# Expert groups: the up product in two halves, additions as two float32r terms, slots released by counts

## The chip, the cores and the metric

The kernel runs on one core of a Trainium2 chip. The metric is the device time of one execution of the whole program, in microseconds (us). The core has TensorE (PE) for matrix products, VectorE (DVE), ScalarE (ACT), GpSimd (POOL), and SyncE (SP), whose queue issues most of the loads from HBM. The loads of all queues are moved by the same 16 DMA engines.

## What is computed

The program is one step of a small diffusion trunk on 384 tokens (128 of a prompt, 256 of a sample) of width 1024, in two layers. Layer 0 mixes tokens by a long convolution, layer 1 by attention. Each is followed by a mixture of 16 experts of 512 hidden units, of which every token uses two, and this is where the change lies:

```python
def _hier_moe(x, w_group, b_group, w_expert, b_expert, w_up, w_down):
    ...
    for e in range(N_EXPERTS):
        a, b = jnp.split(t @ w_up[e], 2, axis=-1)
        y = y + combine[:, e:e + 1] * ((jax.nn.silu(a) * b) @ w_down[e])
    return y.reshape(B, L, D)
```

After the experts of a layer come a residual and a layer norm; layer 1 begins with a modulation by vectors that are a product of a condition with `w_ada`. All data is float32.

## The kernel before

Every engine has its own program, written out by hand, and semaphores order them. The order on each engine is the order of the code.

**Loads.** All large weights go through slots of 2 MB. SP issues them in the order of `LOAD_ORDER`, and each waits until its slot's last user is done. For a layer's experts there are 48 pieces of 2 MB (`MOE_W`): for each expert the two halves of `w_up` over the rows (c = 0, 1) and `w_down` (c = 2). Six ring slots and five places that are free at that time hold 11 pieces, so pieces 0 to 10 are loaded while the stages ahead of the experts still run, and piece i, from 11 on, waits until piece i - 11 has been used. For an up piece that wait (`wait_used`) is for `up_ready`, counted in groups, for a down piece for `expert_done`. `piece` (line 522) and `load` (line 505) issue the transfers. Behind the experts of layer 0 the same slots take `cond7` and `cond8` (two column blocks of `w_ada` for layer 1), then `qkv_4` and so on, through `wait_slot_free`, which waits for `expert_done` too.

**Groups.** The tokens of an expert are dealt out in groups of 32 slots (`SLOT_TOK`); an expert has one or more groups, and `expert` runs a hardware loop over them. In this trace there are 33 groups in each layer. The rows of a group are gathered from HBM by POOL (`group_row`, 128 KB each), turned by DVE into `xgT`. On PE a group is three steps, all through the helper `mm` (line 812):

1. up: 32 float32 products of `xgT` (128x32, held in the array) with 256 columns of `w_up`, in four column strips of the array, into bank 0; the trace shows two instructions for each float32 product, so 64.
2. add (`combine`): the result of the previous group is added to the 384 token rows, which stay in banks 2 to 7. The result is split into three bfloat16 terms (`y3`) whose sum is exact, and multiplied by a 0/1 matrix `ohT` that spreads the slots over the tokens: 3 token tiles x 3 terms x 4 strips = 36 products.
3. down: 16 float32 products (32 instructions) of `heT` with `w_down`, into bank 1.

Between 1 and 3 ACT takes the silu of one half of bank 0 (`gated`, tile `sa`), DVE multiplies it by the other (`he`) and turns it (`heT`). After 3, DVE scales bank 1 by the gates (`yv`) and makes the three terms. After an expert's last group a tiny product (`mm` on `ident`) raises `expert_done`. After the last group `combine_last` adds its result, and the layer norm follows: DVE's statistics (`st`, line 2149), then ACT and DVE on each token tile. In layer 0, ACT's program has the copies of the `cond7` and `cond8` products (`cond_rows_copied`) between these tiles.

## Time and profile before

| what | value |
|---|---|
| time, median of 3 runs | 1043.76 us (1041.48 to 1048.89) |
| span of the profiled execution, first to last instruction | 1041.7 us |
| the fastest timed run, for what lies around the span | 1041.48 us |
| busy: PE, DVE, ACT, POOL | 983.5, 699.0, 189.6, 195.2 us |
| moved from and to HBM | 318.29 MB |
| expert groups: layer 0, layer 1 | about 296 to 517 us, about 791 to 1025 us |

The page gives no other time for the profiled execution than its span, and the fastest timed run is 0.2 us away from it, so the sum is made against 1041.7 us, which is 2.1 us below the median. Lines are those of the kernel before. "Share" of the DMA engines is a mean over 16 of them (the profiler's figure goes slightly over 1), the granted clock is 1.00 at 2.4 GHz and 0.50 at 1.2 GHz.

### The profile page before, as it was taken

The page shows a single profiled execution, that of the slowest core. Times are in us where ns is not written, and L with a number is a line of the kernel's source. Part 1 is how long each engine was busy: PE and PEld are TensorE (multiplying, and loading weights), DVE is VectorE, ACT ScalarE, POOL GpSimd, SP SyncE. Part 2 cuts the span into 40 slices and gives each one's busy share as a digit, 9 for nine tenths or more (in the row PEclk, how much of TensorE's full clock was granted, in tenths as well). Part 3 has the DMA queues.
Part 4 walks back from the last instruction along what each step waited for, and adds up shares of the span by engine and source line. Part 5 has one row for each costly group of instructions (what it writes and reads, how often), then busy time and mean ns, then how long its engine had stood idle before and what let it go on. Part 6 is the DMA issues. An engine that isn't in the chain of part 4 may idle for free.

```text
span 1041.7 us, 28193 instructions
## 1 busy us (share of the span) xinstructions
PE 983.5 (94%) x11412; PEld 583.7 (56%) x11412; DVE 699.0 (67%) x1771; ACT 189.6 (18%) x443; POOL 195.2 (19%) x304
## 2 busy tenths in 40 slices
PE   8999999999899999999899999999989999999783
PEld 2555556565556656666555554575555655666451
DVE  6458884956766666666679995474676666666457
ACT  4342233012310000000140013462231000000003
POOL 1500000620132222222100001254013222222111
PEclk9999999999899999999989999999989999999896
DMA  9964666950999999999997588832097999999991
GB/s 331 400 258 162 221 243 223 389 186 25 344 340 405 405 406 406 405 405 405 393 402 256 213 327 321 289 102 74 5 357 284 374 405 406 405 404 405 407 373 64
DMA packets 102208, 318.29 MB, mean 306 GB/s; under 512 B 8403, under 2 KB 12691, under 8 KB 101748
## 3 DMA queue, kind: packets, MB, share of 16 engines
q1 hardware_dynamic: 92228, 298.87, 74.7%
q0 software_dynamic: 5776, 17.30, 5.0%
q10 hardware_dynamic: 4128, 1.05, 0.4%
q8 instruction: 56, 0.92, 0.4%
q14 instruction: 20, 0.16, 0.0%
HBM read 311.44 MB, written 5.77 MB: 305 GB/s over the span
## 4 chain that ended last, share of the span: by engine, by line
PE 76%; DMA 8%; DVE 6%; SPq 6%; issue 2%; POOL 1%; ACT 1%; DVEq 0%; POOLq 0%
PE bank L812 74%; SPq L522 5%; DMA ring<-in_moe_w_down 4%; DMA ring<-in_w_ada 2%; POOL P L780 1%; PE bank L1320 1%; DVE P L2212 1%; DMA group_row<-token_rows,rows_now 1%; DVE st L2149 0%; PE bank L1027 0%; PE bank L859 0%; ACT x L1514 0%; DVE x L2263 0%; SPq L532 0%; PE bank L871 0%
## 5 line engine op out<-in xcount | busy, mean ns | idle before, releaser
L812 PE MATMUL bank<-ring,xgT 128*32 128x256 f32 x4224 | 244.0, 382 | 7.3 <-DMA ring<-in_moe_w_up 4.9
L812 PE MATMUL bank<-hT,ring 128*128 128x384 f32 x640 | 207.2, 486 | 0.0
L812 PEld LDWEIGHTS bank<-ring,xgT 128*32 128x32 f32 x4224 | 145.5, 111 | 87.6 <-issue 9.5
L812 PEld LDWEIGHTS bank<-hT,ring 128*128 128x128 f32 x640 | 121.4, 190 | 85.6 <-issue 1.8
L1722 DVE CUSTOM_DVE_ANT_0 ring<-ring,ring 128x1024 f32<-128x1024 f32 x112 | 137.1, 1224 | 3.4
L812 PE MATMUL bank<-ring,heT 128*32 128x256 f32 x2112 | 130.3, 386 | 5.3 <-DMA ring<-in_moe_w_down 5.0
L1557 ACT ACTIVATE sa<-bank 128x128 f32<-128x128 f32 x66 | 18.3, 277 | 425.0 <-PE bank L812 425.0
L812 PEld LDWEIGHTS bank<-ring,heT 128*32 128x32 f32 x2112 | 63.5, 110 | 56.4 <-DVE heT L2108 16.1
L2106 DVE TENSOR_TENSOR he<-sa,bank 128x128 f32<-128x128 f32 x66 | 19.0, 288 | 98.5 <-ACT sa L1557 98.5
L812 PE MATMUL bank<-y,ohT 32*128 32x256 bf16 x2448 | 81.3, 271 | 2.6 <-DVE y L2129 1.9
L746 POOL DMA_INDIRECT group_row<-token_rows,rows_now x68 | 74.0, 1088 | 17.6 <-issue 17.3
L812 PEld LDWEIGHTS bank<-y,ohT 32*128 32x128 bf16 x2448 | 56.2, 93 | 36.7 <-issue 27.7
L743 POOL COPY rows_now<-list_i 128x1 int32 (+1 forms) x68 | 12.4, 182 | 321.0 <-DVE xgT L2036 316.0
L2127 DVE TENSOR_TENSOR yv<-bank,slot_gate 128x256 f32<-128x256 f32 x66 | 28.0, 425 | 55.3 <-PE bank L812 55.3
L812 PE MATMUL bank<-ring,hT 128*128 128x512 f32 x96 | 46.8, 623 | 0.0
L812 PE MATMUL bank<-ring,yT 128*128 128x512 f32 x96 | 41.9, 593 | 1.0 <-DVE yT L1875 1.0
L812 PE MATMUL bank<-ring,qT 128*128 128x512 f32 x96 | 42.0, 593 | 0.8 <-DVE qT L2232 0.8
L2118 DVE SCALAR_TENSOR_TENSOR ohT<-pos_all,srow,oh_first 128x384 bf16<-128x384 f32 x66 | 40.4, 612 | 0.2 <-issue 0.2
L684 POOL TENSOR_TENSOR Y<-Y,tmp 128x512 f32<-128x512 f32 x6 | 7.6, 1274 | 145.4 <-DVE tmp L1846 145.1
L1462 ACT ACTIVATE zt<-bank,first 128x128 f32<-128x128 f32 (+1 forms) x48 | 17.5, 416 | 85.4 <-PE bank L812 85.4
L2121 DVE SCALAR_TENSOR_TENSOR slot_gate<-gate_s,slot_weight,slot_gate 128x256 f32<-128x256 f32 x66 | 31.6, 478 | 0.0
L1816 DVE SCALAR_TENSOR_TENSOR acc<-zt,first,acc 128x385 f32<-128x385 f32 x14 | 8.7, 620 | 34.1 <-ACT acc L1452 33.7
(299 smaller groups left out, 1193.8 us busy)
## 6 DMA issues: line engine op xcount, KB each, us to landing
ring<-in_moe_w_up SPq DMA_DIRECT2D x64, 2048.0 KB
ring<-in_moe_w_down SPq DMA_DIRECT2D x32, 2048.0 KB
ring<-in_k_ada SPq DMA_DIRECT2D x14, 2048.0 KB
ring<-in_w_ada SPq DMA_DIRECT2D x10, 2048.0 KB
ring<-in_na_w_qkv SPq DMA_DIRECT2D x6, 2048.0 KB
ring<-in_hy_w_in SPq DMA_DIRECT2D x5, 2048.0 KB
ring<-in_hy_w_out SPq DMA_DIRECT2D x2, 2048.0 KB
ring<-in_na_w_out SPq DMA_DIRECT2D x2, 2048.0 KB
```

The source lines that it names most:

```text
L522: sp.dma_start(w_view(i, 4, 1024), src.rearrange("o (k p) n -> p (o k) n", p=128)).then_inc(w_loaded[W_SLOT[i]], 16)
L743: nc.gpsimd.tensor_copy(rows_now[b][:], list_i[:, column]).then_inc(S["rows_named"], 1)
L746: nc.gpsimd.indirect_dma_start(out=group_row[b][:, :], out_offset=None, in_=token_rows[l][:, :], in_offset=bass.IndirectOffsetOnAxis(ap=ro ...
L780: nc.gpsimd.tensor_scalar_mul(p, p, den[:, 2 * u:2 * u + 1]).then_inc(scaled[0], 1)
L812: return nc.tensor.matmul(out, lhsT, rhs, start=first, stop=last)
L1462: last = nc.scalar.activation(zt[:, n % 2, at_:at_ + b - a], ps[bank_of(g)][:, a:b], ACT.Identity, bias=VT[:, V_BIN + n:V_BIN + n + 1])
L1557: nc.scalar.activation(sa[:], ps[0][:, 0:128], ACT.Silu).then_inc(S["sa_ready"], 1)
L1722: ins = v.tensor_tensor_reduce(scratch, w_view(i, 4, D)[:, q, :], cond_rows(l)[:, c * D:(c + 1) * D], 1.0, 0.0, ALU.mult, ALU.add, mod[l][ ...
L2106: v.tensor_tensor(he[:], sa[:], ps[0][:, 128:256], ALU.mult).then_inc(S["he_ready"], 1)
L2118: v.scalar_tensor_tensor(out=ohT[:].rearrange("p t n -> p (t n)"), in0=pos_all[:, 1, :], scalar=srow[:], in1=oh_first[:], op0=ALU.is_equal ...
L2121: v.scalar_tensor_tensor(out=slot_gate[:], in0=gate_s[:, 1, :], scalar=weight[1], in1=slot_gate[:], op0=ALU.mult, op1=ALU.add).then_inc(S[ ...
L2127: v.tensor_tensor(yv[:], ps[1][:, 0:256], slot_gate[:], ALU.mult).then_inc(S["y_step"], 1)
```

## The change

The inner units of an expert are taken in two halves h. The up product of half h has 128 columns and goes to bank h, so 64 products in place of 32; ACT and DVE handle a half (64 columns) as soon as it is there. Bank 1 is also that of the down product, so half 1 waits until DVE has read the previous group's result (`y_step`), and the down product waits until DVE has read half 1 (`he_ready`); it then starts on the units of half 0 when their `heT` is there. The result is split into two terms in float32r (`yt`) in place of three in bfloat16, and `ohT` becomes float32r too: 24 products in place of 36, and two DVE operations fewer. The tiny product and `expert_done` go; every slot is released by a count of groups (`piece_used`), on `up_ready` or `y_ready`; SP reads a count once for an expert and keeps it. Two tiles are cleared by DVE instead of one by POOL, and PE waits for `srow_ready` ahead of the first group.

```diff
+TERMS, Y_STEPS = 2, 4
-        y3 = at("y3", [128, 3, 256], RM + 10496, b16)
+        yt = at("yt", [128, 2, 256], RK + 3072, f32r)
+        ohT = at("ohT", [128, TT, 128], RM + 10496, f32r)
...
+            def piece_used(l, i):
+                e, c = divmod(i, 3)
+                if e not in groups_through[l]:
+                    count_groups(l, e)
+                if c == 2:
+                    sp.wait_ge(moe_sems[l]["y_ready"], groups_through[l][e])
+                else:
+                    sp.wait_ge(moe_sems[l]["up_ready"], groups_through[l][e] * 2)
...
                     if m <= j < m + MOE_W:
-                        sp.wait_ge(expert_done[l], (j - m) // 3 + 1)
+                        piece_used(l, j - m)
...
+                for e in range(EXPERTS - 4, EXPERTS):
+                    if e not in groups_through[l]:
+                        count_groups(l, e)
...
-                sp.wait_ge(expert_done[l], EXPERTS - 1)
+                piece_used(l, max(i for i in range(MOE_W) if W_SLOT[W_AT[f"moe{l}"] + i] == RING + 2))
...
-                nc.gpsimd.memset(y3[:], 0.0).then_inc(S["y3_ready"], 1)
-                nc.gpsimd.memset(ohT[:], 0.0).then_inc(S["ohT_ready"], 1)
+                nc.gpsimd.memset(ohT[:].bitcast(f32), 0.0).then_inc(S["ohT_ready"], 1)
...
-                        last = mm(bank_at(t, o), ohT[32 * o:32 * o + 32, t, :], y3[32 * o:32 * o + 32, term, :], False,
-                                  end and r + o % 2 >= 2 and term == 2)
+                        last = mm(bank_at(t, o), ohT[32 * o:32 * o + 32, t, :], yt[32 * o:32 * o + 32, term, :], False,
+                                  end and r + o % 2 >= 2 and term == TERMS - 1)
...
-                        for k in range(KT):
-                            if k % 4 == 0:
-                                wait_piece(k // 4)
-                            w = wup[k // 4][:, k % 4, :].rearrange("p (g q n) -> p q g n", q=4, n=32)
-                            for q in range(4):
-                                last = mm(ps[0][32 * q:32 * q + 32, 0:256].rearrange("s (g n) -> s g n", n=32),
-                                          xgT[:, k, :], w[:, q, :, :], k == 0, k == KT - 1)
-                        last.then_inc(S["up_ready"], 1)
+                        for h in range(2):
+                            if h == 1:
+                                pe.wait_ge(S["y_step"], before * Y_STEPS + 3)
+                            for k in range(KT):
+                                if h == 0 and k % 4 == 0:
+                                    wait_piece(k // 4)
+                                w = wup[k // 4][:, k % 4, :].rearrange("p (c h g q n) -> p q h c g n", c=2, h=2, g=2, q=4)
+                                for q in range(4):
+                                    last = mm(ps[h][32 * q:32 * q + 32, 0:128].rearrange("s (c g n) -> s c g n", c=2, g=2),
+                                              xgT[:, k, :], w[:, q, h, :, :, :], k == 0, k == KT - 1)
+                            last.then_inc(S["up_ready"], 1)
-                        pe.wait_ge(S["y3_ready"], w1)
+                        pe.wait_ge(S["yt_ready"], w1)
...
-                        pe.wait_ge(S["heT_ready"], w1)
+                        pe.wait_ge(S["he_ready"], before * 2 + 2)
                         wait_piece(2)
                         for q in range(4):
+                            if q % 2 == 0:
+                                pe.wait_ge(S["heT_ready"], before * 2 + 1 + q // 2)
                             for o in range(4):
                                 last = mm(ps[1][32 * o:32 * o + 32, 0:256], heT[:, 32 * q:32 * q + 32],
-                    mm(ps[0][0:2, 0:2], ident[:, 0:2], ident[:, 0:2]).then_inc(expert_done[l], 1)
...
                 pe.wait_ge(nb_ready, l + 1)
+                pe.wait_ge(S["srow_ready"], 1)
...
                 def gated(g):
-                    act.wait_ge(S["up_ready"], g + 1)
-                    nc.scalar.activation(sa[:], ps[0][:, 0:128], ACT.Silu).then_inc(S["sa_ready"], 1)
+                    for h in range(2):
+                        act.wait_ge(S["up_ready"], g * 2 + 1 + h)
+                        nc.scalar.activation(sa[:, 64 * h:64 * h + 64], ps[h][:, 0:64], ACT.Silu).then_inc(S["sa_ready"], 1)
...
+                v.memset(yt[:].bitcast(f32), 0.0).then_inc(S["yt_ready"], 1)
+                v.memset(credit[:, 2:3], 0.0).then_inc(S["y_step"], Y_STEPS)
...
+                def half_gated(g, h):
+                    cols_of = slice(64 * h, 64 * h + 64)
+                    dve.wait_ge(S["sa_ready"], g * 2 + 1 + h)
+                    v.tensor_tensor(he[:, cols_of], sa[:, cols_of], ps[h][:, 64:128], ALU.mult).then_inc(S["he_ready"], 1)
+                    dve.wait_ge(S["he_ready"], g * 2 + 1 + h)
+                    v.transpose(heT[:, cols_of], he[:, cols_of]).then_inc(S["heT_ready"], 1)
...
+                    step = g * Y_STEPS + Y_STEPS
+                    half_gated(g, 0)
                     dve.wait_ge(S["srow_ready"], g + 1)
                     v.tensor_scalar(oh_first[:], pos_all[:, 0, :], srow[:], None, ALU.is_equal).then_inc(S["oh_first_ready"], 1)
                     weight = [slot_weight[:, c, bass.ds(g, 1)] for c in range(2)]
                     v.tensor_scalar(slot_gate[:], gate_s[:, 0, :], weight[0], None, ALU.mult).then_inc(S["y_step"], 1)
+                    half_gated(g, 1)
+                    dve.wait_ge(S[f"rows{b}_in"], count * 16)
+                    turned(group_row[b][:])
...
                     v.tensor_tensor(yv[:], ps[1][:, 0:256], slot_gate[:], ALU.mult).then_inc(S["y_step"], 1)
-                    dve.wait_ge(S["y_step"], g * 6 + 3)
-                    v.tensor_copy(y3[:, 0, :], yv[:]).then_inc(S["y_step"], 1)
-                    dve.wait_ge(S["y_step"], g * 6 + 4)
-                    v.tensor_tensor(yv[:], yv[:], y3[:, 0, :], ALU.subtract).then_inc(S["y_step"], 1)
-                    dve.wait_ge(S["y_step"], g * 6 + 5)
-                    v.tensor_copy(y3[:, 1, :], yv[:]).then_inc(S["y_step"], 1)
-                    dve.wait_ge(S["y_step"], g * 6 + 6)
-                    v.tensor_tensor(y3[:, 2, :], yv[:], y3[:, 1, :], ALU.subtract).then_inc(S["y3_ready"], 1)
+                    dve.wait_ge(S["y_step"], step + 3)
+                    v.tensor_copy(yt[:, 0, :], yv[:]).then_inc(S["y_step"], 1)
+                    dve.wait_ge(S["y_step"], step + 4)
+                    v.tensor_tensor(yt[:, 1, :], yv[:], yt[:, 0, :], ALU.subtract).then_inc(S["yt_ready"], 1)
```

How PE's instructions stand in an expert's loop (layer 0, second expert; `ring_53` and `ring_56` are its up pieces, `ring_49` its down piece; ISA, REGISTER_ALU and branches are the sequencer's). Before:

```order
L812 MATMUL bank<-ring_53,xgT 32x256 x16
L812 MATMUL bank<-ring_56,xgT 32x256 x16
L812 MATMUL bank<-y_136,ohT 128x256 x24
L1106 ISA
L812 MATMUL bank<-y_136,ohT 128x256 x12
L812 MATMUL bank<-ring_49,heT 32x256 x16
L1144 REGISTER_ALU
L1144 COMPARE_AND_BRANCH
L812 MATMUL bank<-first 2x2
```

After:

```order
L823 MATMUL bank<-ring_53,xgT 32x128 x16
L823 MATMUL bank<-ring_56,xgT 32x128 x16
L1160 ISA
L823 MATMUL bank<-ring_53,xgT 32x128 x16
L823 MATMUL bank<-ring_56,xgT 32x128 x16
L823 MATMUL bank<-yt,ohT 128x256 x16
L1117 ISA
L823 MATMUL bank<-yt,ohT 128x256 x8
L1173 ISA
L1177 REGISTER_ALU
L823 MATMUL bank<-ring_49,heT 32x256 x16
L1155 REGISTER_ALU
```

The up product now stands twice, with 128 columns in place of 256, the additions are 24 in place of 36, the tiny product behind the loop is gone, and sequencer instructions with a wait stand ahead of half 1 and of the down product.

DVE's instructions of one group (layer 0, the second group; `y_136` is `y3`). Before:

```order
L2106 TENSOR_TENSOR he<-sa,bank 128x128
L2108 STREAM_TRANSPOSE heT<-he 128x128
L2036 STREAM_TRANSPOSE xgT<-group_row_130 128x256
L2113 TENSOR_SCALAR oh_first<-pos_all,srow 128x384
L2115 TENSOR_SCALAR slot_gate<-gate_s,slot_weight 128x256
L2118 SCALAR_TENSOR_TENSOR ohT<-pos_all,srow,oh_first 128x384
L2121 SCALAR_TENSOR_TENSOR slot_gate<-gate_s,slot_weight,slot_gate 128x256
L2123 TENSOR_SCALAR srow<-srow 128x1
L2127 TENSOR_TENSOR yv<-bank,slot_gate 128x256
L2129 CAST y_136<-yv 128x256
L2131 TENSOR_TENSOR yv<-yv,y_136 128x256
L2133 CAST y_136<-yv 128x256
```

After:

```order
L2126 TENSOR_TENSOR he<-sa,bank 128x64
L2128 STREAM_TRANSPOSE heT<-he 128x64
L2135 TENSOR_SCALAR oh_first<-pos_all,srow 128x384
L2137 TENSOR_SCALAR slot_gate<-gate_s,slot_weight 128x256
L2126 TENSOR_TENSOR he<-sa,bank 128x64
L2128 STREAM_TRANSPOSE heT<-he 128x64
L2053 STREAM_TRANSPOSE xgT<-group_row_130 128x256
L2144 SCALAR_TENSOR_TENSOR ohT<-pos_all,srow,oh_first 128x384
L2147 SCALAR_TENSOR_TENSOR slot_gate<-gate_s,slot_weight,slot_gate 128x256
L2149 TENSOR_SCALAR srow<-srow 128x1
L2153 TENSOR_TENSOR yv<-bank,slot_gate 128x256
L2155 CAST yt<-yv 128x256
```

The multiplication and the turn come in two pieces, with two operations on slot numbers between them; the turn of the next group's rows (`xgT`) stands behind the second piece; the splitting behind `yv` is two operations shorter.

SP's queue at the end of the experts of layer 0, where the first load behind them is `cond7` (`in_w_ada`); TENSOR_LOAD reads a count of groups. Before:

```order
L522 ISA
L522 DMA ring_52<-in_moe_w_up 128x4x1024
L532 TENSOR_LOAD NBi
L532 ISA x2
L522 ISA
L522 DMA ring_53<-in_moe_w_down 128x4x1024
L505 DMA ring_49<-in_w_ada 128x8x512
```

After:

```order
L489 TENSOR_LOAD NBi
L489 ISA x2
L500 REGISTER_ALU
L539 ISA
L539 DMA ring_53<-in_moe_w_down 128x4x1024
L489 TENSOR_LOAD NBi
L489 ISA x2
L489 TENSOR_LOAD NBi
L489 ISA x2
L489 TENSOR_LOAD NBi
L489 ISA x2
L522 DMA ring_49<-in_w_ada 128x8x512
```

Three counts are read between the last expert piece and the load of `cond7`; the order of the loads themselves is as before.

## Rows read from the trace of the kernel before

**Rows 1.** The page: busy time, share of the span and instructions of each engine.

```profile
PE 983.5 (94%) x11412; PEld 583.7 (56%) x11412; DVE 699.0 (67%) x1771; ACT 189.6 (18%) x443; POOL 195.2 (19%) x304
```

**Rows 2.** Windows, expert stages: length, busy time by engine; last, clock, DMA share, GB/s.

```profile
300.00:520.00 220.00, 216.11 (x4380) 132.43 (x4376) 145.55 (x435) 10.96 (x36) 47.44 (x97) 1.00 1.03 404
810.00:1012.00 202.00, 193.14 (x3834) 117.15 (x3825) 124.59 (x375) 8.04 (x29) 41.59 (x85) 0.97 1.02 405
799.00:809.00 10.00, 9.98 (x216) 5.92 (x208) 7.17 (x23) 0.55 (x2) 1.66 (x5) 1.00 0.14 39
```

**Rows 3.** The chain that ended last, in order of time: start, length, what.

```profile
495.37 25.58 DMA ring<-in_w_ada
521.09 3.81 PE bank L812 x32
...
989.13 23.81 DMA ring<-in_moe_w_down
```

**Rows 4.** Timeline, PE in late layer 1: start, length, [idle before and what ended it].

```profile
927.82 3.66 PE L812 MATMUL bank<-ring,xgT 128*32 128x256 f32 x64
931.41 1.16 PE L812 MATMUL bank<-y,ohT 32*128 32x256 bf16 x36
932.53 1.93 PE L812 MATMUL bank<-ring,heT 128*32 128x256 f32 x32
934.28 3.64 PE L812 MATMUL bank<-ring,xgT 128*32 128x256 f32 x64
...
940.74 0.19 PE L812 MATMUL bank<-first 128*2 128x2 f32 x2
...
970.37 3.27 PE L812 MATMUL bank<-ring,xgT 128*32 128x256 f32 x32 [2.82 <-DMA ring<-in_moe_w_up]
...
997.04 3.59 PE L812 MATMUL bank<-ring,heT 128*32 128x256 f32 x32 [2.53 <-DMA ring<-in_moe_w_down]
...
1013.08 1.93 PE L812 MATMUL bank<-ring,heT 128*32 128x256 f32 x32 [1.42 <-DMA ring<-in_moe_w_down]
```

**Rows 5.** Timeline, ACT and DVE in the first of these groups.

```profile
931.54 0.28 ACT L1557 ACTIVATE sa<-bank 128x128 f32<-128x128 f32 x1 [6.41 <-PE bank L812]
931.85 0.29 DVE L2106 TENSOR_TENSOR he<-sa,bank 128x128 f32<-128x128 f32 x1 [1.36 <-ACT sa L1557]
932.17 0.31 DVE L2108 STREAM_TRANSPOSE heT<-he 128x128 f32<-128x128 f32 x1
...
935.15 0.42 DVE L2127 TENSOR_TENSOR yv<-bank,slot_gate 128x256 f32<-128x256 f32 x1 [0.79 <-PE bank L812]
```

**Rows 6.** PE's rows nearest to the new shapes: timeline, chain, groups by form.

```profile
763.64 1.08 PE L812 MATMUL bank<-first,mod 128*32 128x128 f32 x32
...
36.19 2.68 PE bank L851 x24
...
L812 PEld LDWEIGHTS bank<-y,ohT 32*128 32x128 bf16 x2448 | 56.2, 93 | 36.7 <-issue 27.7 <-PE bank L812 2.8 <-DVE y L2129 2.1
```

**Rows 7.** Timeline, SP's queue: start, length of the issue.

```profile
488.61 12.16 SPq L505 DMA_DIRECT2D ring<-in_w_ada  x2
...
807.33 0.37 SPq L522 DMA_DIRECT2D ring<-in_moe_w_down  x1
```

**Rows 8.** ACT behind layer 0's experts (timeline); two stretches with a low clock (windows).

```profile
521.00 1.45 ACT L1514 ACTIVATE x<-bank,sd 128x512 f32<-128x512 f32 x2 [0.55 <-DVE sd L1889]
...
523.07 0.60 ACT L1386 ACTIVATE arow<-bank 128x512 f32<-128x512 f32 x1 [0.62 <-PE bank L812]
...
526.00:533.00 7.00, 6.24 (x16) 3.46 (x15) 4.70 (x18) 4.43 (x11) 0.00 (x0) 0.51 1.02 407
998.00:1000.00 2.00, 2.00 (x24) 1.00 (x20) 0.00 (x0) 0.00 (x0) 0.00 (x0) 0.50 1.03 410
```

**Rows 9.** Timeline, DVE on the third term of layer 1's last group.

```profile
1022.86 0.29 DVE L2133 CAST y<-yv 128x256 bf16<-128x256 f32 x1
1023.19 0.43 DVE L2135 TENSOR_TENSOR y<-yv,y 128x256 bf16<-128x256 f32 x1
```

More of the change, by code:

```diff
@@ L220, in build @@
 def build(nc, A, y_prompt, y_sample, new_k, new_v):
-    f32, i32, b16 = mybir.dt.float32, mybir.dt.int32, mybir.dt.bfloat16
+    f32, i32, b16, f32r = mybir.dt.float32, mybir.dt.int32, mybir.dt.bfloat16, mybir.dt.float32r
     ACT = mybir.ActivationFunctionType
@@ L379, in build @@
         w_loaded = [sem(f"w_loaded{r}") for r in range(RING + EXTRA)]
-        expert_done = [sem(f"expert_done{l}") for l in range(DEPTH)]
         group_ready = sem("group_ready")
@@ L418, in build @@
                 "oh_pair", "oh_ready", "gathered", "picks_ready", "list_summed", "list_ready", "hot_ready", "picks_step", "rows_named", "rows_stored", "x_added", "rows0_in", "rows1_in", "xgT_ready", "up_ready", "sa_ready",
[L419 removed]
+                "he_ready", "heT_ready", "y_ready", "y_step", "yt_ready", "oh_first_ready", "ohT_ready", "srow_ready", "combined")})
         block = ctx.enter_context(nc.Block())
@@ L483, in last_group, with count_groups @@
                         return G_AT["qk"] + 4 * s + 3 if s < 4 else G_AT["v_01" if s == 4 else "v_12"]
+            groups_through = [{}, {}]
+            def count_groups(l, e):
+                groups = sp.value_load(NBi[0:1, NB_CUM + 1 + e:NB_CUM + 2 + e], min_val=1, max_val=MAX_BLOCKS)
+                groups_through[l][e] = whole_pairs(groups) if e == EXPERTS - 1 else groups
+            def piece_used(l, i):
[6 more added lines that the diff above has]
+                    sp.wait_ge(moe_sems[l]["up_ready"], groups_through[l][e] * 2)
             def wait_slot_free(i):
@@ L525, in experts @@
                 S = moe_sems[l]
-                def wait_used(i):
-                    e, c = divmod(i, 3)
-                    if c == 2:
-                        sp.wait_ge(expert_done[l], e + 1)
-                    else:
-                        groups = sp.value_load(NBi[0:1, NB_CUM + 1 + e:NB_CUM + 2 + e], min_val=1, max_val=MAX_BLOCKS)
-                        sp.wait_ge(S["up_ready"], groups)
                 for i in range(MOE_W):
@@ L548, in experts @@
                     if i >= RING + EXTRA:
-                        wait_used(i - RING - EXTRA)
+                        piece_used(l, i - RING - EXTRA)
                     elif slot < RING:
@@ L1106, in combine @@
                             pe.wait_ge(S["combined"], done)
-                        for term in range(3):
+                        for term in range(TERMS):
                             last = add_term(r, term)
@@ L1113, in combine_last @@
                 def combine_last(total):
-                    for term in range(3):
-                        if term < 2:
-                            pe.wait_ge(S["y_step"], total * 6 + 2 * term - 2)
+                    for term in range(TERMS):
+                        if term < TERMS - 1:
+                            pe.wait_ge(S["y_step"], total * Y_STEPS + 2 * term + 4)
                         else:
-                            pe.wait_ge(S["y3_ready"], total + 1)
+                            pe.wait_ge(S["yt_ready"], total + 1)
                         if term > 0:
@@ L1125, in combine_last @@
                             last = add_term(r, term, True)
-                            if term < 2 or r == 0:
+                            if term < TERMS - 1 or r == 0:
                                 last.then_inc(S["combined"], 1)
@@ L2101, in moe @@
                 total = dve.value_load(NBi[0:1, NB_ALL:NB_ALL + 1], min_val=EXPERTS, max_val=MAX_BLOCKS)
-                def group(g, b, count):
-                    dve.wait_ge(S["sa_ready"], g + 1)
-                    v.tensor_tensor(he[:], sa[:], ps[0][:, 128:256], ALU.mult).then_inc(S["he_ready"], 1)
-                    dve.wait_ge(S["he_ready"], g + 1)
-                    v.transpose(heT[:], he[:]).then_inc(S["heT_ready"], 1)
-                    dve.wait_ge(S[f"rows{b}_in"], count * 16)
-                    turned(group_row[b][:])
+                def half_gated(g, h):
[4 more added lines that the diff above has]
+                    v.transpose(heT[:, cols_of], he[:, cols_of]).then_inc(S["heT_ready"], 1)
+                def group(g, b, count):
+                    step = g * Y_STEPS + Y_STEPS
+                    half_gated(g, 0)
                     dve.wait_ge(S["srow_ready"], g + 1)
@@ L2119, in group @@
                                            in1=oh_first[:], op0=ALU.is_equal, op1=ALU.add).then_inc(S["ohT_ready"], 1)
-                    dve.wait_ge(S["y_step"], g * 6 + 1)
+                    dve.wait_ge(S["y_step"], step + 1)
                     v.scalar_tensor_tensor(out=slot_gate[:], in0=gate_s[:, 1, :], scalar=weight[1], in1=slot_gate[:],
```

6 lines of the change are left out of this document (2 added, 4 removed).

## The prediction

> **What bounds the kernel now.** I read the page's busy shares first, then the chain, then the expert stages by windows, and last PE and SP in order of time. The page makes PE the bound: it is busy 94% of the span [rows 1]. The windows of the two expert stages say otherwise. From 300 to 520 us and from 810 to 1012 us all 16 DMA engines are busy without a gap (share 1.03 and 1.02, 404 and 405 GB/s), while PE is busy for 216.1 of 220 and 193.1 of 202 us [rows 2]. Both are full; what counts is which of them the end waits for. The chain names it twice: cond8, a load behind the expert pieces of layer 0, from 495.37 to 521.09, and the last expert piece of layer 1 from 989.13 on [rows 3]. SP shows why these take 24 and 26 us, for 2 MB, which at 405 GB/s take 5.2: each is in a queue behind others. cond7 and cond8 are issued at 488.61, with the issue itself held up for 12.16 us [rows 7], so the slot was free long before the engines came to it. And at the end of layer 1 PE stands in front of pieces that have not landed: 2.82 us at 970, 2.53 at 997, 1.42 at 1013 [rows 4].
>
> The bytes give the same end. In layer 1 the engines are nearly idle from 799 to 809 (share 0.14) [rows 2], because piece 11 may not be issued before the third group of the first expert is through its up product, at 807.33 [rows 7]. From there 37 pieces of 2.097 MB and 33 gathers of 0.131 MB are 81.9 MB, 202 us at 405 GB/s: from 810 to 1012, and the last down product starts at 1013.08 [rows 4]. So PE's work in the expert stages is paid for only where it releases piece 11, and behind the last piece.
>
> **The change, part by part.** Take the group of rows 4 at 927.82: up to 931.41 (3.59 us), additions to 932.53 (1.12), down to 934.28 (1.75), together 6.46; after an expert's last group the tiny product adds 0.19, which over 16 experts and 33 groups is 0.09 a group. PE's work in a layer is 33 x 6.55 = 216 us.
>
> *Up in halves.* The same columns, in twice as many instructions. The nearest row has the shape of a half exactly: a 128x32 operand held, 128 columns moving, float32; 32 of them take 1.08 us [rows 6], and with some 0.28 for one to run through that is 26 ns each. 128 of them are 0.28 + 127 x 0.026 = 3.6 us, as the 64 before (3.66) [rows 4]. I take 0; bounds -0.1 and +0.3 (64 more instructions with 5 ns of overhead).
> *Half 1 waits for bank 1.* The wait is for `yv`, which in these rows ends at 935.57, 1.29 us after the up product began at 934.28 [rows 4, 5]; half 1 begins 1.8 us after it. Queued behind it on PE are half 1, the additions and the down product, and behind those ACT and DVE; 0.5 us of margin, so 0.
> *Two terms.* 24 products instead of 36, at the pace of the 36 (1.16 us with 0.27 for the last to run through: 25 ns each) 0.85 us, 0.3 less [rows 4]. No row shows a float32r product. From below it is bounded by that; from above by loading the held operand, 128 columns of float32, one after the other: transposes with such an operand take 2.68 us for 24 [rows 6]. I take 0.85: the strips of the additions lie in different rows of the array, and the bfloat16 loads take 93 ns each where 36 of them go through in 1.16 us, so they do overlap by strip [rows 4, 6].
> *The down product's start.* Before, it waits for `heT`, ready at 932.48, when the additions end, too [rows 4, 5]. Now the additions would end 0.3 earlier, at 932.24; half 1's `he` is ready by 0.28 + 0.29 and two hand-overs after 931.54, at 932.14 even if 64 columns took as long as 128, and half 0's `heT` is long there. Down follows the additions; 0.3 gained. DVE has two operations more for the halves (at most 0.6 us) and 0.72 us fewer for the third term [rows 5, 9]; it doesn't matter.
> *The tiny product and the counts.* -0.09 a group on PE. SP reads three counts ahead of cond7's load; the queue it feeds runs some 25 us behind, as the 12.16 us of held-up issue show [rows 7]: 0. Were the queue empty, each such read would show in full.
> *The start.* PE now reads the first group's count only when `srow` is there, behind the list that it waited for anyhow; I allow 0.5 us (0 to 0.8) in each layer. In layer 0 the gather of the second group covers it.
>
> Together PE needs about 6.46 - 0.3 - 0.09 = 6.1 us a group, 13 us less in each layer. Where does that go? **Layer 0:** nothing. cond8 lands at 521.09 whenever PE is done, its DMA engines being full since 300 us with the same pieces in the same order, and ACT, which must copy cond8's product, takes that up at 523.07, 0.6 us after it was free (521.00 + 1.45) [rows 8]. What is late next is cond8 itself. **Layer 1, piece 11:** start +0.5, two groups at -0.3 ahead of the third up product: 0 (-0.6 to +0.8), and all later pieces move by that. **Behind the last piece:** of a down product, one full group and the last additions remain: one set of additions (-0.3), and in `combine_last` the third term's cast and subtraction, 0.29 + 0.43, with their hand-overs 0.8 [rows 9]. Sum: -1.1 us, 1041.7 to 1040.6 in the profiled execution, and from the median 1043.76 to **1042.7**. Edges: -0.6 and -1.1 more if the halves are quicker, +2 below.
>
> **A rule that speaks against the change.** The rows say that loads of bfloat16 operands overlap by strip. The Trainium skill (TensorE: Matmul & The Clock Gate, Weight-path perf modes) says that the fast load of weights is on for 128 weights of a type that isn't FP32 and gains nothing for fp32; its section on LDWEIGHTS gives P/1.2 ns for P columns. By that page, as an estimate, 24 loads one after the other would be 24 x 107 ns = 2.6 us. No run here shows a float32r load; what it would do is the first rival.
>
> **The rivals.** *Serial loads: slower.* If the float32r additions are held up by their loads as in the transposes, they take 2.68 us instead of 1.16: +1.52 - 0.09 = +1.43 a group, 47 us a layer. Layer 0 has 0.6 us to spare, so +46; layer 1 takes it out of its waits for pieces (2.82, 2.53, 1.42 and two smaller, together 9.4) [rows 4], so +38. About 1126 us. It decides from +0.3 us a group on (additions of 1.6 us), where 1% is lost: 33 x 0.33 = 11 in layer 0. Against it: the overlap above. At half the pace (57 ns each, as the float32 instructions of the up product [rows 4]) they'd be 1.37 us, +0.15 a group, and only layer 0 would pay: 1046.
> *A lower clock.* PE will wait longer for pieces, and behind such waits rows show half the clock: the granted clock is 0.51 (1.2 GHz) from 526 to 533 and 0.50 from 998 to 1000 [rows 8], where the down product begun at 997.04, behind a wait of 2.53 us, takes 3.59 us instead of 1.93 [rows 4]. A stretch of 4 us at half the clock in front of the end costs 2 us, one more behind layer 0 another 2: 1047. For it: PE is ahead more often. Against: the wait in front of the very last piece grows by little, since the up pieces of the same expert land just ahead of it.
> By the Trainium skill (the same page, HAM oscillation), a PE that waits for each tile's load falls back to half rate each time; the trace agrees behind the wait at 997.
> *PE is the bound after all: faster.* If the full DMA engines only followed PE's releases, both layers would give 13 us: 1018. For it: PE's 94% and its share of the chain. Against it: PE's own waits for pieces, and issues held up for 12 us.
> *The change doesn't do what it says:* a wait (bank 1, `he`) uses up the 0.3 us. Then the end is where it was, 1043 to 1044, since PE isn't waited for.
>
> **How the numbers follow.** About 1% (10.4 us) is what a measurement of this kernel can tell from no change. Chances: hidden as forecast, the last rival with it, 0.68; lower clock 0.12; additions or halves moderately slower (1.2 to 1.6 us; 1046 to 1058) 0.09; serial loads 0.06; PE the bound 0.05. Over 1% slower: serial loads and most of the moderate case, 0.13. Over 1% faster: 0.05. The rest, 0.82, is within 1%. The range leaves out serial loads and PE as the bound, and the upper part of the moderate case: 1038 to 1052; it needs no more below, because nothing in the sum beyond -2.5 has a place in the chain, and the runs differ by some us.
>
> **What would show it.** In the profile after: additions of 24 products at 0.8 to 0.9 us and groups of about 6.1 us where no piece is waited for; DMA share at 1.02 in both expert stages, over about the same length; more waits of PE for `ring` pieces, from about 490 us on in layer 0 and 930 in layer 1; cond8's product at 521 and the last piece at 1013, each within 1 us; two terms behind the last group. I am wrong if groups take over 6.8 us, or if the engines' full stretch gets shorter, which would mean that the bytes did not set it.

## The result, and the profile after

The changed kernel takes 1101.1 us (median of four runs), the kernel before, measured beside it, 1042.7: ratio 1.0535, 95% interval 1.0487 to 1.0584, so 5.4% slower. One run of 1972.7 us lies far off the others and is not in the ratio. The profiled execution has a span of 1100.0 us, 58.3 more than before. The forecast was 1042.7 us, 1038 to 1052; that this is also the time of the kernel before is chance.

The page of the changed kernel: busy time and instructions by engine; the queue that carries the engines' code (packets, MB, share); the chain by engine; PE's groups (busy, mean ns | idle before them, and what ended it).

```profile
PE 997.7 (91%) x14756; PEld 674.1 (61%) x14756; DVE 677.4 (62%) x1775; ACT 200.9 (18%) x509; POOL 210.1 (19%) x302
...
q8 instruction: 69, 1.13, 0.4%
...
PE 86%; issue 6%; DVE 6%; POOL 1%; ACT 1%; DMA 0%; SPq 0%; DVEq 0%; ACTq 0%
...
L823 PE MATMUL bank<-ring,xgT 128*32 128x128 f32 x8448 | 256.2, 276 | 37.1 <-issue 36.8
...
L823 PE MATMUL bank<-ring,heT 128*32 128x256 f32 x2112 | 141.2, 395 | 18.7 <-issue 18.7
```

Against [rows 1], PE is busy only 14 us longer, with 3344 more instructions, but idle 44 us longer: 102.3 us of the span instead of 58.2. Of its idle time 55.5 us (36.8 + 18.7) are stops in the middle of up and down products, a few just ahead of one, in which PE waits for nothing that the profile shows ("issue"); before, these two groups had 1.7 us of them. In return the waits for loads that the two groups had before, 9.9 us, are gone.

PE's timeline around the end of layer 0: start, length, [idle before and what ended it].

```profile
497.75 1.49 PE L823 MATMUL bank<-ring,heT 128*32 128x256 f32 x21
499.66 1.05 PE L823 MATMUL bank<-ring,heT 128*32 128x256 f32 x11 [0.41 <-issue]
501.20 3.26 PE L823 MATMUL bank<-ring,xgT 128*32 128x128 f32 x112 [0.49 <-issue]
507.77 1.08 PE L823 MATMUL bank<-ring,xgT 128*32 128x128 f32 x16 [3.30 <-issue]
508.78 1.68 PE L823 MATMUL bank<-yt,ohT 32*128 32x256 f32 x24
510.38 2.20 PE L823 MATMUL bank<-ring,heT 128*32 128x256 f32 x32
512.41 3.67 PE L823 MATMUL bank<-ring,xgT 128*32 128x128 f32 x128
516.01 1.09 PE L823 MATMUL bank<-yt,ohT 32*128 32x256 f32 x24
517.03 1.93 PE L823 MATMUL bank<-ring,heT 128*32 128x256 f32 x32
518.78 3.68 PE L823 MATMUL bank<-ring,xgT 128*32 128x128 f32 x128
```

The up product that starts at 501.20 is an expert's first pass through its loop. It stops for 3.30 us after 112 of its 128 products, where no semaphore stands. The passes at 512.41 and 518.78 run the same instructions without a stop: up 3.60, additions 1.02, down 1.75, together 6.37 us (before 6.46 [rows 4]). It is so everywhere: stops in the first pass of an expert, where the code is new, none in later ones. The stops also sit at a fixed distance in the code: 11 down and 112 up products, 123 in all, lie between the one at 499.66 and the one at 507.77, and from one such expert to the next the place moves by one or two products.

The DMA windows of the changed kernel (columns as in [rows 2]): a stop, the products behind it, and three stretches of layer 0.

```profile
504.50:507.70 3.20, 0.00 (x0) 0.00 (x0) 0.04 (x1) 0.00 (x0) 0.00 (x0) 0.98 1.03 404
507.80:512.40 4.60, 4.60 (x72) 3.06 (x76) 1.87 (x6) 0.22 (x1) 1.49 (x3) 0.65 1.04 417
...
400.00:410.00 10.00, 10.00 (x284) 8.08 (x280) 6.61 (x22) 0.45 (x2) 3.47 (x6) 1.00 0.25 91
450.00:460.00 10.00, 10.00 (x272) 7.62 (x266) 5.98 (x21) 0.67 (x3) 3.41 (x6) 1.00 0.23 59
540.00:550.00 10.00, 9.37 (x223) 7.09 (x223) 4.48 (x16) 0.67 (x3) 1.70 (x3) 0.83 0.24 85
```

During the stop the DMA engines are full; behind it PE's clock is granted at 0.65 and the additions take 1.68 us instead of 1.09. And the engines, which before were full from 300 to 520 [rows 2], now run dry three times (59 to 91 GB/s), because a late PE frees its slots late: between 300 and 520 us SP's queue waits for PE for 112.8 us, before for 53.3. What the DMA queue moved during the stop (queue, packets, MB, share of the 16 engines):

```profile
q1 hardware_dynamic: 313, 1.28, 100.4%
q8 instruction: 1, 0.02, 2.1%
```

One packet of code, at 2.1% of 16 engines for 3.2 us about 1.1 us long, beside 313 packets of weights. By its record in the trace it moved from 505.25 to 506.32 us, and PE went on 1.45 us later. That is the rule: of the 41 stops marked issue in the two expert stages (55.4 us in all), 34 with 51.0 us end 1.2 to 1.6 us after a packet of code has landed. Of the other seven, five of 0.3 to 0.5 us follow closely on such a stop, ahead of the next up product. The last two, 1.23 and 1.02 us, stand ahead of the first group of each layer; every kernel here with the other parts of the change has these two (1.0 to 1.2 us), while the kernel before has 0.39 and 0.21 us there.

The piece of the chain behind layer 0, before and after, and PE's windows from the first up product of layer 0 to its last addition, before and after (columns as in [rows 2]):

```profile
535.33 104.40 PE bank L812 x312
581.55 104.40 PE bank L823 x312
...
296.00:517.60 221.60, 217.78 (x4425) 134.41 (x4424) 143.43 (x429) 11.13 (x36) 49.15 (x100) 1.00 1.02 401
296.00:562.60 266.60, 232.93 (x6096) 183.32 (x6096) 131.46 (x429) 16.30 (x68) 55.80 (x100) 0.95 0.89 345
```

So layer 0 loses 46 us, and all behind it 12. The groups of layer 0 take 45 us longer; in 30 of them PE is idle, in 15 it is busy, at a mean clock of 0.95.

### The profile page after: what moved, and what is told of

Same layout as the page of the kernel before. It is cut to its first block, busy times and chain, and to the rows that moved or that the text cites. A ratio compares the mean times of both kernels' runs of the same rounds, so it can differ in the third digit from the quotient of the medians.

```text
span 1100.0 us, 35122 instructions
## 1 busy us (share of the span) xinstructions
PE 997.7 (91%) x14756; PEld 674.1 (61%) x14756; DVE 677.4 (62%) x1775; ACT 200.9 (18%) x509; POOL 210.1 (19%) x302
## 3 DMA queue, kind: packets, MB, share of 16 engines
q8 instruction: 69, 1.13, 0.4%
## 4 chain that ended last, share of the span: by engine, by line
PE 86%; issue 6%; DVE 6%; POOL 1%; ACT 1%; DMA 0%; SPq 0%; DVEq 0%; ACTq 0%
PE bank L823 83%; POOL P L791 1%; PE bank L1335 1%; DVE P L2234 1%; DVE st L2171 1%; PE bank L1038 0%; PE bank L870 0%; ACT x L1529 0%; DVE x L2285 0%; PE bank L882 0%; DVE x L2286 0%; PE bank L862 0%; DMA dabs<-in_hy_decay 0%; DVE hT L1922 0%; DVE sc L1984 0%
## 5 line engine op out<-in xcount | busy, mean ns | idle before, releaser
L823 PE MATMUL bank<-ring,xgT 128*32 128x128 f32 x8448 | 256.2, 276 | 37.1 <-issue 36.8
L823 PEld LDWEIGHTS bank<-ring,xgT 128*32 128x32 f32 x8448 | 237.9, 111 | 60.6 <-issue 55.4
L823 PE MATMUL bank<-ring,heT 128*32 128x256 f32 x2112 | 141.2, 395 | 18.7 <-issue 18.7
L2126 DVE TENSOR_TENSOR he<-sa,bank 128x64 f32<-128x64 f32 x132 | 29.2, 221 | 146.1 <-ACT sa L1574 146.1
L1574 ACT ACTIVATE sa<-bank 128x64 f32<-128x64 f32 x132 | 29.6, 224 | 471.1 <-PE bank L823 471.1
L754 POOL COPY rows_now<-list_i 128x1 int32 (+1 forms) x68 | 25.9, 381 | 369.5 <-DVE xgT L2053 364.6
L823 PE MATMUL bank<-yt,ohT 32*128 32x256 f32 x1632 | 78.7, 322 | 2.1 <-DVE yt L2155 1.9
L823 PEld LDWEIGHTS bank<-yt,ohT 32*128 32x128 f32 x1632 | 60.5, 193 | 20.5 <-issue 13.9
L2144 DVE SCALAR_TENSOR_TENSOR ohT<-pos_all,srow,oh_first 128x384 fp32r<-128x384 f32 x66 | 40.6, 615 | 2.9 <-PE bank L823 2.9
L2128 DVE STREAM_TRANSPOSE heT<-he 128x64 f32<-128x64 f32 x132 | 32.4, 246 | 4.5
```

The source lines that it names most:

```text
L754: nc.gpsimd.tensor_copy(rows_now[b][:], list_i[:, column]).then_inc(S["rows_named"], 1)
L823: return nc.tensor.matmul(out, lhsT, rhs, start=first, stop=last)
L1574: nc.scalar.activation(sa[:, 64 * h:64 * h + 64], ps[h][:, 0:64], ACT.Silu).then_inc(S["sa_ready"], 1)
L2126: v.tensor_tensor(he[:, cols_of], sa[:, cols_of], ps[h][:, 64:128], ALU.mult).then_inc(S["he_ready"], 1)
L2128: v.transpose(heT[:, cols_of], he[:, cols_of]).then_inc(S["heT_ready"], 1)
L2144: v.scalar_tensor_tensor(out=ohT[:].rearrange("p t n -> p (t n)"), in0=pos_all[:, 1, :], scalar=srow[:], in1=oh_first[:], op0=ALU.is_equal ...
```

## The experiments

**The theory.** PE's code is fetched in blocks of some 16 KB (1.13 MB in 69 packets), the next, I take it, while the present one runs. Each expert has code of its own, and its loop runs one to five times; in layer 0 ten of the 16 experts have a single group. A first pass runs through code that is new: before, 64 up, 36 addition and 32 down pairs (load and multiply), 132; after, 128, 24 and 32, 184. In layer 0, with the engines full of weights, 6.3 to 8.1 us pass from the end of one stop behind a packet to the end of the next (499.66 to 507.77), which I take for the time of a block. The half-width up product runs through its instructions twice as fast, 128 pairs in 3.6 us, so it comes to the end of a block before the next is there. **The rivals:** the new hand-overs, the float32r terms, or the counts hold PE up.

**Up in one piece.** The two terms and the counts stay.

```diff
-for h in range(2):                      # 128 pairs of 128 columns, banks 0 and 1
-    ... xgT[:, k, :], w[:, q, h, :, :, :] ...; last.then_inc(S["up_ready"], 1)
+for k in range(KT):                     # 64 pairs of 256 columns, bank 0
+    ... xgT[:, k, :], w[:, q, :, :] ...
+last.then_inc(S["up_ready"], 2)
-sa[:, 64 * h:64 * h + 64] = Silu(ps[h][:, 0:64])
+sa[:] = Silu(ps[0][:, 0:128])
```

> The changed kernel with the up product in one piece again (64 load and multiply pairs of 256 columns in bank 0, one hand-over to ScalarE; the two float32r terms, the release by counts, DVE's work in halves stay). Theory: PE stalls because the code of an expert's first pass comes in too slowly; an expert now has 64 + 24 + 32 = 120 pairs instead of 184 (132 before), so the stalls marked issue go, and the time is that of the kernel before: 1041, between 1037 and 1047. Rival, the float32r terms or the counts hold PE up: the time stays at 1095 to 1102, since both are still there.

Measured: 1075.3 us, ratio 1.0319 (1.0272 to 1.0366). Neither number. The groups of PE (columns as above):

```profile
L823 PE MATMUL bank<-ring,xgT 128*32 128x256 f32 x4224 | 241.0, 380 | 3.2 <-issue 2.5
...
L823 PE MATMUL bank<-ring,heT 128*32 128x256 f32 x2112 | 129.2, 386 | 53.0 <-DVE he L2122 50.7
```

The stops are gone (36.8 to 2.5 us), as the theory has it. But a fault of my edit came in their place: DVE still gated half 1 behind the one-hot and the slot gate, which only pays when half 1 comes later from PE, and the down product waited 50.7 us for `he`. So the time of this run says nothing on the terms and the counts; the third experiment takes the fault out.

**More code, and nothing else.** The kernel before, its up product in 128 pairs, one bank, one hand-over.

```diff
+for h in range(2):
     for k in range(KT): ... for q in range(4):
-        mm(ps[0][32 * q:32 * q + 32, 0:256], xgT[:, k, :], w[:, q, :, :], ...)
+        mm(ps[0][32 * q:32 * q + 32, 128 * h:128 * h + 128], xgT[:, k, :], w[:, q, h, :, :], ...)
```

> The kernel before with one edit: its up product is issued as 128 pairs of 128 columns instead of 64 of 256, into the same bank, with the same single hand-over. Nothing else changes, no wait is added. Theory of the code: 196 pairs per expert instead of 132, more than the changed kernel's 184, so it is at least as slow as that: 1100 to 1120, with stalls marked issue in the first pass of each expert only. Rival, the waits of the new hand-overs or the new terms cost the time: 1042 to 1047, since the products themselves keep their pace (3.68 us for either form).

Measured: 1111.5 us, ratio 1.0652 (1.0611 to 1.0694): slower than the changed kernel, with none of its hand-overs, terms or counts. Its timeline on PE, in a first pass and the next:

```profile
423.96 0.50 PE L812 MATMUL bank<-y,ohT 32*128 32x256 bf16 x10
426.74 0.94 PE L812 MATMUL bank<-y,ohT 32*128 32x256 bf16 x26 [2.28 <-issue]
427.61 1.94 PE L812 MATMUL bank<-ring,heT 128*32 128x256 f32 x32
429.36 3.68 PE L812 MATMUL bank<-ring,xgT 128*32 128x128 f32 x128
432.97 1.16 PE L812 MATMUL bank<-y,ohT 32*128 32x256 bf16 x36
```

The stop falls into the additions here, which this edit doesn't touch: it follows the place in the code, not the operation. None of the three rivals is in this kernel, so none of them is needed for the loss.

**Terms and counts without halves.** As the first, with ScalarE's and DVE's gating in one operation each, ahead of the one-hot.

```diff
-half_gated(g, 0); ...; half_gated(g, 1)
+he[:] = sa[:] * ps[0][:, 128:256]; heT[:] = transpose(he[:])   # then rows, one-hot, slot gate
```

> The kernel before with two parts of the change: two float32r terms in place of three bfloat16 ones, and the release by counts in place of the tiny product; the up product in one piece, and ScalarE and DVE gate its 128 columns in one operation each, ahead of the one-hot, as before. 120 pairs of instructions per expert. Theory: the 50.7 us for which PE waited for he in the run with one up product came from the gating in halves behind a single hand-over and go; stalls marked issue stay at some 3 us; the time is that of the kernel before, bound by the loads: 1036 to 1045. Rival, the terms or the counts cost something themselves: 1050 to 1075.

Measured: 1054.7 us, ratio 1.0113 (1.0095 to 1.013): above the theory's range and inside the rival's. Its PE timeline in a steady group:

```profile
421.09 3.64 PE L823 MATMUL bank<-ring,xgT 128*32 128x256 f32 x64
424.65 1.09 PE L823 MATMUL bank<-yt,ohT 32*128 32x256 f32 x24
425.99 1.93 PE L823 MATMUL bank<-ring,heT 128*32 128x256 f32 x32 [0.25 <-DVE heT L2124]
427.74 3.64 PE L823 MATMUL bank<-ring,xgT 128*32 128x256 f32 x64
```

No stops (3.6 us of issue in all), but `heT` is 0.25 us late behind the shorter additions, and a group takes 6.65 us. PE waits 18.1 us for it in all; whether the 11 us are this hand-over is what the next experiment tests. The halves remove this wait: in the changed kernel the down product never waits for `heT`.

**The same with `he` turned in two halves.**

```diff
-v.transpose(heT[:], he[:]).then_inc(S["heT_ready"], 2)
+for h in range(2): v.transpose(heT[:, 64 * h:64 * h + 64], he[:, 64 * h:64 * h + 64]).then_inc(S["heT_ready"], 1)
-pe.wait_ge(S["he_ready"], before * 2 + 2)      # not needed with bank 0 alone
```

> The one-piece version with two float32r terms and counts once more, with one difference: DVE turns he in two halves, so that the first half of the down product can start after the first half is turned. In the run with both in full, PE waited 0.24 us a group for heT, 18.1 us in all, because the shorter additions end before heT is ready; its groups took 6.66 us. Theory: the code is no longer the limit (120 pairs per expert), the hand-over is; turned in halves it is shorter by 0.1 to 0.2 us a group, groups of 6.45 to 6.55 us, and the time is 1043 to 1051, at or just above the kernel before. Rival, the 11 us by which the version in full was slower lie elsewhere (the counts, the first groups): 1053 to 1056 again.

PE's wait for `he_ready` is gone too, which the expectation doesn't name; DVE makes `heT` from `he`, so the wait for `heT` covers it.

Measured: 1047.2 us, ratio 1.0035 (1.0019 to 1.005), inside the theory's range. Its steady groups take 6.52 us, without a wait that the timeline would mark:

```profile
416.96 3.64 PE L823 MATMUL bank<-ring,xgT 128*32 128x256 f32 x64
420.53 1.09 PE L823 MATMUL bank<-yt,ohT 32*128 32x256 f32 x24
421.73 1.93 PE L823 MATMUL bank<-ring,heT 128*32 128x256 f32 x32
423.48 3.64 PE L823 MATMUL bank<-ring,xgT 128*32 128x256 f32 x64
```

So two terms and counts cost some 3 us (2 to 5), and bring nothing. No version here that loads all its weights beats the kernel before.

**Long code for every second expert.** The edit of the second experiment under `if e % 2 == 1`.

> The kernel before with the up product in 128 pairs of 128 columns for every second expert (196 pairs of code) and as it was for the others (132). With all experts at 196 the kernel took 68 us more than before, 2.1 us per expert. Theory without credit: each long expert costs its 2.1 us, 16 x 2.1 = 34, so 1077 (1070 to 1084). Rival, the code is fetched ahead and a short expert behind a long one makes good what was lost, so that it decides how much code there is on average: 1044 to 1062.

Measured: 1071.5 us, ratio 1.025 (1.0229 to 1.0271), +27 us: at the low end of the theory's range (1070 to 1084) and outside the rival's. Stops come to 29.7 us, half of those with all experts long.

**Loads halved in layer 1, after and before.**

```diff
-piece(first + i, up[who, c * 512:(c + 1) * 512, :] ...)
+n = 256 if l == 1 and i >= RING + EXTRA else 512
+piece(first + i, up[who, c * 512:c * 512 + n, :] ..., n // 128)
```

> The changed kernel, but in layer 1 the expert pieces from the 12th on load half of their rows (the other half of a slot keeps what an earlier piece left there, so the output of layer 1's experts differs); layer 0 is as it was. The DMA engines then carry about half of the bytes in that stage. Theory, a block of code waits behind the weight loads: in layer 1 the stalls marked issue shrink from some 27 us to under 8, single ones to under 1 us, and the stage runs at PE's pace, about 33 x 6.4 = 211 us. Rival, the stalls belong to the number of instructions or to the sequencer whatever the DMA engines do: single stalls of 1 to 3 us stay, 20 us or more in layer 1. Layer 0 keeps its stalls under both.

> The kernel before with the same half loads in layer 1 (from the 12th piece on; the output of layer 1's experts differs). Theory: layer 1 runs at PE's pace, 33 x 6.55 = 216 us of work, so with the changed kernel's light run beside it the pure saving on PE is read: 2 to 5 us in favour of the changed kernel in layer 1. Rival, the changed kernel's stalls don't depend on the loads: it is still 20 us slower in that stage.

Measured, one run each: 1089.1 and 1030.1 us. They gained 12 and 14 us in all, and the gap stayed 59. But 7.2 of the 12 us lie ahead of layer 1, where the edit changes nothing: the piece of the chain behind layer 0 begins at 574.35 in this run instead of 581.55 (534.39 instead of 535.33 in the other). Behind that point the changed kernel gained 5.5 us and the kernel before 12.5, and the gap there grew from 12 to 19 us. Layer 1's stops shrank from 22.2 only to 18.7 us. By what I had written this spoke for the rivals: the stops, and some 20 us in that stage, stay whatever the loads do. The next run says otherwise.

**Almost no loads in layer 1.** As before, with 128 rows of 64 columns, 32 KB, a piece.

> The changed kernel, but in layer 1 the expert pieces from the 12th on load 32 KB instead of 2 MB (the output of layer 1's experts differs); the DMA engines then carry almost only the gathers of tokens and PE's code in that stage. Halving the loads took layer 1's stalls marked issue only from 22.2 to 18.7 us. Theory, code comes in blocks, and a block takes long by itself, the loads add to it: stalls of 0.9 to 1.1 us remain at the places where they were 0.95 to 1.01 in both runs (104 pairs into an expert's code), and those of 1.6 to 2.8 us shrink by a half or more; 8 to 15 us in layer 1. Rival 1, only the full DMA engines delay the code: all stalls under 0.3 us, under 4 us in all. Rival 2, the stalls aren't a transfer at all: 18 to 22 us stay.

Measured, one run: 1071.2 us. Layer 1's window on this kernel:

```profile
850.00:950.00 100.00, 100.00 (x2879) 82.46 (x2875) 62.43 (x205) 7.16 (x32) 26.69 (x47) 1.00 0.11 29
```

The only two stops that are left there, in PE's timeline:

```profile
835.48 3.70 PE L825 MATMUL bank<-ring,xgT 128*32 128x128 f32 x128 [1.03 <-issue]
...
1026.74 0.86 PE L825 MATMUL bank<-ring,xgT 128*32 128x128 f32 x23 [1.22 <-issue]
```

2.25 us instead of 22.2, with the same code: rival 1 of this run, that only the loads delay the code, comes nearest, and my own theory's 8 to 15 us was wrong. The first of the two is the one ahead of a layer's first group, the second comes behind 6 us with a share of 0.65. From 850 to 950 ten packets of code came in, and PE is busy for 100.00 of 100 us.

With half of the bytes the stops nearly stay, with 1.6% of them they go. The run with half loads shows why: its engines are empty on the mean, but not where new code is entered. Its windows in layer 1 (columns as above): the stage, two of the stops, and a stretch without one.

```profile
830.00:1060.00 230.00, 211.48 (x5872) 171.28 (x5876) 125.92 (x412) 14.30 (x64) 55.95 (x98) 1.00 0.57 207
895.90:897.20 1.30, 0.03 (x1) 0.00 (x0) 0.37 (x2) 0.00 (x0) 0.00 (x0) 1.00 1.00 375
980.20:981.20 1.00, 0.00 (x0) 0.00 (x0) 0.04 (x1) 0.00 (x0) 0.00 (x0) 1.00 1.01 414
920.00:940.00 20.00, 20.00 (x592) 16.62 (x584) 12.59 (x43) 1.34 (x6) 5.19 (x9) 1.00 0.27 91
```

In 16 of its 18 stops in layer 1 the share is above 0.9 during the stop.

**What the code waits behind.** Descriptors of 2 KB instead of 4 (two DMAs a piece), and at most two pieces under way:

```diff
+for m in range(2): sp.dma_start(w_view(i, 4, 1024)[:, :, cols_of], ...[:, :, cols_of])     # first run
+sp.wait_ge(w_loaded[W_SLOT[i - 2]], 16 * W_COUNT[i - 2])                                 # second run
```

> The changed kernel with each expert piece loaded by two DMAs of 512 columns, so that the descriptors are of 2 KB instead of 4 KB; the same bytes in the same order. If a block of code waits behind a number of load descriptors that are already taken up, it waits behind half of the bytes, and the stalls of layer 0 (1.2 to 3.3 us each) shrink to half or less: 1060 to 1085. If it waits for its share of the engines, or by itself, nothing changes (1095 to 1105); smaller descriptors may also move fewer bytes per us, which would show as a rate below 404 GB/s and a longer time.

> The changed kernel, but SyncE issues an expert piece (from the 12th of a layer on) only when the piece two before it has landed, so at most two pieces, 4 MB, are in the DMA queue instead of four or five. If a block of code waits behind all that is queued on its engine, blocks come in faster (under 5 us instead of 6.3 to 8.1) and the stalls of layer 0 shrink by a half or more: 1060 to 1085. If code and loads take turns, the length of the queue is no matter: the stalls stay and the time is 1095 to 1110.

Measured, one run each: 1105.0 and 1090.9 us. Smaller descriptors leave the stops as they were (33.7 us in layer 0, 33.2 without), but full engines move less with them: 384 GB/s from 320 to 340 us instead of 405. With the shorter queue the stops only go from 33.2 to 30.7 in layer 0 and from 22.2 to 19.4 in layer 1. That the 10 us of this run are its doing is not shown: the piece of the chain behind layer 0 begins 7 us earlier than in the changed kernel, but so it did in the run with half loads, whose layer 0 is unchanged. So neither the number of descriptors nor the length of the queue is most of the wait, and how code and loads share an engine stays open.

**All of it in one table.** Pairs of code per expert, packets of code on the page, PE's idle rows marked issue added up (timeline from 296 to 560 and from 780 to 1090 us), and the ratio to before:

| kernel | pairs | packets | stops, us | ratio |
|---|---|---|---|---|
| one piece, `he` turned in halves | 120 | 52 | 2.2 + 1.8 | 1.0035 |
| before | 132 | 56 | 1.4 + 0.7 | 1 |
| every second expert long | 164 | 64 | 13.0 + 16.7 | 1.025 |
| changed | 184 | 69 | 33.2 + 22.2 | 1.0535 |
| before, all experts long | 196 | 72 | 28.1 + 28.0 | 1.0652 |

The packets follow the code. The last row has 64 pairs, 128 instructions, more in each of 32 experts than before: 4096 instructions and 16 packets, 256 to a packet. With 16.4 KB in a packet that is 64 bytes each, and about 123 pairs between two stops fit it, with the waits and loop instructions of PE. In the first row most of the stops are the two ahead of a layer's first group (1.23 and 1.17 us).

The Trainium skill (Runtime: NRT & Kernel Launch, Instruction fetch mechanics) says that code is fetched in blocks of 16 KiB, 256 instructions, the next during the present one, and that the cost of crossing is "mostly hidden". The size agrees with the packets here. "Mostly hidden" agrees with the kernels of 120 and 132 pairs and with the run without loads in layer 1, but not with the changed kernel, where 55.5 us are open.

## Why the prediction was wrong

**The step that failed** is *Up in halves*: "I take 0; bounds -0.1 and +0.3 (64 more instructions with 5 ns of overhead)". Its steady cost is right: 3.68 us against 3.66, and down and additions follow at once (no row gives the 5 ns). But I priced instructions by what they take in a loop that has already run, and never asked for the code of a first pass. By the second experiment 64 more pairs alone cost 67 us, where the sum had none. There was a sign in the trace of before, in rows that I passed over as issue: two short stops once layer 0 was under way, one ahead of an up product and one in the middle of a down product.

```profile
441.16 3.66 PE L812 MATMUL bank<-ring,xgT 128*32 128x256 f32 x64 [0.38 <-issue]
...
447.26 1.27 PE L812 MATMUL bank<-ring,heT 128*32 128x256 f32 x18 [0.33 <-issue]
```

The second ends 1.56 us after a packet of code has landed. A group of 132 pairs takes 6.5 us there, so a block of 123 about 6.1, an estimate, just under the 6.3 to 8.1 from stop to stop in the changed kernel: the kernel before was at the edge. What a block takes to come in its trace did not give. That pairs of half the width run through a block in 3.6 us, and so ask for code almost twice as fast, could have been worked out.

**"Layer 0: nothing"** fell with it. The reasoning holds while PE is no later than the loads; the version with 120 pairs that turns `he` in halves shows it (402 GB/s from 300 to 520, time within 0.5%). But layer 0 had no room: before, PE was busy for 216.1 of 220 us there [rows 2]. The stops make PE late by 33 us, and then the loads wait for PE. The sign named for it came: from 300 to 520 us the engines' share is 0.92 instead of 1.03. Layer 1, where PE had 9.4 us of waits for pieces [rows 4], has 22.2 us of stops, and all behind layer 0 lost only 12 us.

**Lower clock**, a rival at 2 us a stretch, came on a larger scale: behind the stop of 3.30 us the clock is 0.65 over 4.6 us, and from 296 to 562.6 us it is 0.95 (before 1.00 from 300 to 520 [rows 2]). 5% of 267 us is 13 us, an estimate, and the windows show PE busy for 15 us more in layer 0's groups. The other 30 of the 45 us there are idle time: 33 us of stops, less the waits that the kernel before had. The rival's condition, longer waits for pieces, did not come.

**Two terms:** 0.85 us forecast, 1.09 measured, both with the last product to run through (1.02 without). They are not serial, as the rival feared, and not as quick as bfloat16: 24 in 1.02 us, 42 ns each, against 31 (36 in 1.12), with loads of the held operand of 193 ns (PEld on the page) against 93 [rows 6]. The changed kernel's group gained 0.09 (6.46 to 6.37) beside the tiny product, not 0.3.

**The start:** 0.5 us forecast in each layer, 0.8 measured (1.23 and 1.02 us ahead of the first groups instead of 0.39 and 0.21).

**Half 1 waits for bank 1, the down product's start:** right, neither waits. **The counts on SP:** right, as far as the version that turns `he` in halves shows it (+3 us in all). **Serial loads, PE as the bound, and a change without effect:** the first and last did not come. PE did become the bound, but from being slower. The prediction had that for the additions alone, in serial loads; that its +46 us for layer 0 is the measured number is luck, since the additions were not what slowed PE.

## What to carry to other kernels

Count instructions also as code: where each expert has code of its own that runs only one to five times, each pass through new code costs its fetch, and instructions that are half as wide ask for it twice as fast. Compare the time in which an engine runs through a block of 256 instructions with what such a block takes to come in while the DMA engines are full, here 4.6 (changed) and 6.1 us (before) against 6.3 to 8.1. Look for short "issue" stops in the middle of a product, in first passes only: they say that the edge is near. And read the engines' share at the stops, not over the stage: a mean of 0.57 hid full engines at nearly every stop.

A bound by bytes protects a slower engine only as far as that engine waits; here it stood idle for 4 us of 220 in layer 0.

## What the runs showed of the hardware

PE's code travels on the DMA engines beside the weights, in packets of 16.4 KB. With the engines full (share 1.03) a first pass stood still for up to 3.3 us, although the packet itself took about 1.1; with the share at 0.11 the same code ran without a stop for 100 us, in which ten packets of it came in. PE went on 1.2 to 1.6 us after a packet had landed. Half of the load bytes took only a sixth off the stops, since the engines were full at them all the same. Descriptors of 2 KB instead of 4 left the stops as they were, and full engines moved 384 GB/s instead of 405 (one run). Passes through code that has once been run had no stop, though an expert's loop is longer than one block: from 346 to 370 us, the second to the fifth pass of an expert, no packet of code moved.
